# First mixer's output norm in a two-block layer: pairs of squares added on VectorE, one-column sums moved behind the last product, constant matmuls on TensorE around the norms

## The reference

```python
def rms_norm(x, g):
    y = x * rsqrt(mean(x * x, axis=-1) + EPS)
    return y * g

merged = sigmoid(ga) * y_conv + sigmoid(gb) * y_attn
mix_out = merged @ w_out                                  # 1024 x 1024
x = x + gt1 * rms_norm(mix_out, g_post_mix)               # first norm of this stretch
h2 = rms_norm(x, g_pre_mlp) * (1.0 + sc2) + sh2           # second norm of this stretch
ff = square(relu(h2 @ w_mlp_in)) @ w_mlp_out
x = x + gt2 * rms_norm(ff, g_post_mlp)
...                                                       # then the second layer
```

## Time and profile before

| | |
|---|---|
| median of 3 runs | 819.95 us (818.74 to 822.18) |
| the profiled execution | 821.43 us |
| its span, first to last instruction | 819.7 us |
| TensorE matmuls busy | 767.8 us, 94% |
| VectorE busy | 523.6 us, 64% |
| ScalarE busy | 379.1 us, 46% |
| mean granted TensorE clock | 0.948 of full speed |

### The profile page before, as it was taken

One profiled execution on the slowest core, in us unless ns is written; L12 is line 12 of the kernel. 1 busy time (PEld: TensorE's weight loads), 2 busy tenths in 40 slices (PEclk: granted clock), 3 DMA queues, 4 the chain that ended last, 5 costly groups with the idle time before them and its releaser, 6 DMA issues.

```text
span 819.7 us, 14006 instructions
## 1 busy us (share of the span) xinstructions
PE 767.8 (94%) x6051; PEld 731.6 (89%) x6051; DVE 523.6 (64%) x706; ACT 379.1 (46%) x520; POOL 68.7 (8%) x68
## 2 busy tenths in 40 slices
PE   3599999999979999999998999899799999999997
PEld 3499989999979999999997997687489999999997
DVE  4887677687346776644436898967655676555441
ACT  3453443543433555553434445577653554443441
POOL 1500111001000000000001000004000222221000
PEclk9599999999869999999998988999799999999999
DMA  8979666785413886575651451241606476654511
GB/s 343 364 255 338 200 208 210 249 272 194 152 52 112 254 272 201 193 240 172 205 162 52 155 157 50 62 145 52 205 9 198 136 226 204 205 190 147 192 40 52
DMA packets 123826, 146.01 MB, mean 178 GB/s; under 512 B 3988, under 2 KB 114804, under 8 KB 123764
## 3 DMA queue, kind: packets, MB, share of 16 engines
q1 hardware_dynamic: 122400, 143.32, 53.3%
q10 hardware_dynamic: 1364, 1.79, 0.6%
HBM read 144.05 MB, written 1.05 MB: 177 GB/s over the span
## 4 chain that ended last, share of the span: by engine, by line
PE 71%; DVE 16%; issue 5%; ACT 4%; DMA 2%; POOL 1%; POOLq 0%; SPq 0%; ACTq 0%; DVEq 0%
PE bank L576 59%; DVE w_lo L1420 4%; DVE mod_acc L1412 3%; ACT w_hi L1030 2%; DVE wide L1715 2%; PE bank L622 2%; DMA raw<-in_w_ada 2%; PE bank L603 1%; DVE score L1776 1%; DVE neg_max L1781 1%; PE bank L786 1%; PE bank L815 1%; PE bank L801 1%; PE bank L611 1%; PE bank L873 1%
## 5 line engine op out<-in xcount | busy, mean ns | idle before, releaser
L1420 DVE TENSOR_TENSOR w_lo<-raw,w_hi 128x2048 fp32r<-128x2048 f32 (+1 forms) x108 | 243.7, 2261 | 139.3 <-ACT w_hi L1030 139.2
L1030 ACT ACTIVATE w_hi<-raw 128x2048 fp32r<-128x2048 f32 (+1 forms) x110 | 206.5, 1883 | 230.8 <-PE bank L576 209.1
L576 PE MATMUL bank<-act_hi,w_hi 128*128 128x256 f32 x816 | 235.1, 288 | 5.6 <-ACT act_hi L1186 2.7
L576 PE MATMUL bank<-act_lo,w_hi 128*128 128x256 f32 x816 | 232.5, 285 | 0.7 <-DVE act_lo L1680 0.4
L576 PE MATMUL bank<-act_hi,w_lo 128*128 128x256 f32 x816 | 231.9, 284 | 1.3 <-DVE w_lo L1420 1.3
L576 PEld LDWEIGHTS bank<-act_hi,w_hi 128*128 128x128 f32 x816 | 159.0, 195 | 9.3 <-issue 8.2
L576 PEld LDWEIGHTS bank<-act_lo,w_hi 128*128 128x128 f32 x816 | 159.0, 195 | 1.9 <-DVE act_lo L1680 0.7
L576 PEld LDWEIGHTS bank<-act_hi,w_lo 128*128 128x128 f32 x816 | 158.5, 194 | 1.9 <-DVE w_lo L1420 1.9
L576 PE MATMUL bank<-hidden_hi,w_hi 128*128 128x256 f32 x432 | 121.3, 281 | 1.3 <-DVE wide L1980 1.3
L576 PE MATMUL bank<-hidden_hi,w_lo 128*128 128x256 f32 x432 | 121.1, 280 | 0.0
L576 PE MATMUL bank<-hidden_lo,w_hi 128*128 128x256 f32 x432 | 121.1, 280 | 0.0
(11 more groups left out here) (265 smaller groups left out, 974.5 us busy)
## 6 DMA issues: line engine op xcount, KB each, us to landing
raw<-in_w_in SPq DMA_DIRECT2D x31, 1024.0 KB, 5.8
raw<-in_w_ada SPq DMA_DIRECT2D x24, 1024.0 KB, 6.8
raw<-in_w_gate_up SPq DMA_DIRECT2D x22, 1024.0 KB, 5.1
raw<-in_w_mlp_in SPq DMA_DIRECT2D x16, 1024.0 KB, 5.4
raw<-in_w_mlp_out SPq DMA_DIRECT2D x16, 1024.0 KB, 5.4
raw<-in_w_out SPq DMA_DIRECT2D x8, 1024.0 KB, 6.9
raw<-in_w_down SPq DMA_DIRECT2D x8, 1024.0 KB, 5.0
raw<-in_w_down SPq DMA_DIRECT2D x4, 768.0 KB, 4.3
```

What stands on the lines that cost most here:

```text
L576: i = e.matmul(dst, lhs, rhs, start=start and k == 0 and m == 0 and n == 0, stop=stop and k == kt - 1 and n == 2, skip_group_check=True)
L1030: e.activation(w_hi[slot][:, 0:kt * n_cols], raw[i % N_RAW][:, 0:kt * n_cols], ACT.Copy).then_inc(hi_split, 1)
L1420: e.tensor_tensor(w_lo[slot][:, 0:kt * n_cols], raw[i % N_RAW][:, 0:kt * n_cols], w_hi[slot][:, 0:kt * n_cols].bitcast(F32), ALU.subtract) ...
```

## The change

The sums between products OUT1 + 2 and OUT1 + 3 are gone. VectorE adds the squares of pair 1 to those of pair 0 (`add_to_first(1)`, ahead of a w_lo split), and those of pair 2 on top (`add_to_first(2)`, behind that split); each addition is over 128 x 512 and raises `pair_added`. After product OUT1 + 3 TensorE sums pair 0, once both additions are made, and pair 3. `keep_busy` multiplies the identity by itself, 128 columns wide, into the first 128 columns of the bank that product MLP1 will start anew: eight times after the first spreading, once after each of the four pair sums of the second norm, five times after the second spreading. The results are not read. The count that `ffn_sums` waits for in the second layer is raised by the two additions.

```diff
--- before.py
+++ after.py
@@ -613,16 +613,24 @@
                 if last:
                     i.then_inc(sums_done, 1)
 
-            def sum_columns(i, n):
+            def sum_columns(i, n, ready=None):
 
                 pe.wait_ge(consts, 3)
-                pe.wait_ge(squared, squared_by[n] + i)
+                if ready is not None:
+                    pe.wait_ge(*ready)
+                else:
+                    pe.wait_ge(squared, squared_by[n] + i)
                 for tt in range(TT):
                     for k in (2 * i, 2 * i + 1):
                         t = e.matmul(bank[SUMS][:, tt:tt + 1], squares[:, k, tt * P:(tt + 1) * P], mean_of[:],
                                      start=k == 0 and tt == 0, stop=k == DT - 1, skip_group_check=True)
                 if i == DT // 2 - 1:
                     t.then_inc(col_summed, 1)
+
+            def keep_busy(n, o):
+
+                for _ in range(n):
+                    e.matmul(o[:, 0:P], ident[:], ident[:], start=True, stop=True, skip_group_check=True)
 
             def spread_rstd(n):
 
@@ -726,20 +734,22 @@
             modulation_sum(SHIFT2)
             modulation_sum(SCALE2)
             product(OUT1 + 2, start_bank(OUT1 + 2), act_hi, act_lo, ready_merged)
+            product(OUT1 + 3, start_bank(OUT1 + 3), act_hi, act_lo, ready_merged)
             pe.wait_ge(rms_set, 1)
-            sum_columns(0, 0)
-            sum_columns(1, 0)
-            product(OUT1 + 3, start_bank(OUT1 + 3), act_hi, act_lo, ready_merged)
-            sum_columns(2, 0)
+            sum_columns(0, 0, ready=(pair_added, DT // 2 - 2))
             sum_columns(3, 0)
             spread_rstd(0)
+            o, o1 = start_bank(MLP1), start_bank(MLP1 + 1)
+            keep_busy(8, o)
             pe.wait_ge(col_rms, 1)
             for i in range(DT // 2):
                 sum_columns(i, 1)
+                keep_busy(1, o)
             spread_rstd(1)
-
-
-            two_products(MLP1, start_bank(MLP1), start_bank(MLP1 + 1), act_hi, act_lo, ready_h2)
+            keep_busy(5, o)
+
+
+            two_products(MLP1, o, o1, act_hi, act_lo, ready_h2)
             for p in range(MLP1 + 2, MLP2):
                 product(p, start_bank(p), act_hi, act_lo, ready_h2)
                 if p == GATE2_SUM_AFTER:
@@ -953,7 +963,7 @@
 
 
             def ffn_sums(i):
-                sum_tiles((2 * i,), i == 0, i == DT // 2 - 1, (pair_added, i + 1))
+                sum_tiles((2 * i,), i == 0, i == DT // 2 - 1, (pair_added, DT // 2 - 2 + i + 1))
 
             for i in range(DT // 2):
                 product(OUT2 + i, start_bank(OUT2 + i), act_hi, act_lo, ready_mix2)
@@ -1591,6 +1601,13 @@
             dve.wait_ge(mod_set, 3)
             e.tensor_tensor(gain1[:], mod[:, GATE1 * DT:(GATE1 + 1) * DT], cols("g_post_mix", 0, DT), ALU.mult).then_inc(gains_set, 1)
 
+            def add_to_first(i):
+
+                dve.wait_ge(squared, squared_by[0] + i)
+                dve.wait_ge(pair_added, i - 1)
+                e.tensor_tensor(squares[:, 0:2, :], squares[:, 0:2, :], squares[:, 2 * i:2 * i + 2, :],
+                                ALU.add).then_inc(pair_added, 1)
+
             def add_pair(i, n_squared):
                 dve.wait_ge(squared, n_squared)
                 e.tensor_tensor(squares[:, 2 * i, :], squares[:, 2 * i, :], squares[:, 2 * i + 1, :],
@@ -1604,7 +1621,9 @@
             e.tensor_scalar(scale2[:], mod[:, SCALE2 * DT:(SCALE2 + 1) * DT], 1.0, None, ALU.add).then_inc(gains_set, 1)
             dve.wait_ge(gains_set, 4)
             e.tensor_tensor(scale2[:], scale2[:], cols("g_pre_mlp", 0, DT), ALU.mult).then_inc(gains_set, 1)
+            add_to_first(1)
             low_after(product_at[OUT1 + 2])
+            add_to_first(2)
 
             def column_reciprocal(n):
                 dve.wait_ge(col_rms, n + 1)
```

## The result

Over 15 runs of each kernel, taken on the same chips, the changed kernel takes 816.17 us in the median (813.88 to 819.81) against 821.32 (818.61 to 826.10). The ratio is 0.994 with a 95% interval of 0.992 to 0.996: faster by .6%, or some 4.9 us (3.3 to 6.6). Forecast were 3.45 us less, 816.5, in a range of 813.0 to 819.4. That 816.5 and 816.17 meet is in part luck: the forecast started from 819.95, the median of 3 runs before, which over 15 runs is 1.4 us higher, and the measured change is larger than the forecast one by about as much. The prediction also held a gain within .5% for likelier (.55) than one above it (.41); .6% came. The two profiled executions differ by 5.3 us (816.13 and 821.43), so their traces can stand for the medians.

The account below looks back on a forecast made before the run. TensorE's queue was taken to bound the kernel (71% of the chain). Terms -1.70 - 1.1 + .7 - 1.35 = -3.45 us, from the median of 819.95 to 816.5 us; 8-in-10 range 813.0 to 819.4.

Parts of the forecast that it names:

- step 1: Between the last two projections: the one-column sums leave TensorE's queue, -1.70 us in full.
- step 2: Two VectorE additions, .68 us each, around the w_lo split: no cost, .5 us of cover for the second.
- Rival D: Additions on VectorE come late and TensorE waits: up to +.7 us on any case; no own chance, folded into bounds.
- steps 3 and 4: Second norm: eight constants after the first spread free at full clock; with singles, sums end earlier, -1.1 us (+1.3 to -2.4).
- step 5: Before the MLP: five constants at half clock, the product queued behind them, +.7 us.
- step 6: MLP's first two products: clock returns about 2.1 us into the product instead of 5.0, -1.35 us.
- The bound of -2.1: MLP's first two products: the most they could gain, at full clock from the start, -2.1 us.
- Kept behind: After the MLP's first products: the gain is kept, splits and loads move along, VectorE's split has 4 us of cover.
- Rival A: Clock holds at full from the first norm into the MLP: -6.7 us, 813.2 us; chance .22.
- Rival B: Only the removed sums count, constants' cost paid back by the earlier return: -1.70 us, 818.2 us; chance .15.
- Rival C: Constants are a load, clock falling before or in the eight: net +1.25 us, 821.2 us; chance .15.

Follow-up runs that it names:

- experiment 11: Changed kernel without the two VectorE additions, TensorE summing all four pairs behind the last projection: 819.03 us, ratio .9976 to the kernel before.
- experiment 2: Kernel before plus the constants alone (eight, one after each pair, five), sums left between the last two products: 818.95 us, ratio .9979.
- 7: Changed kernel with the second modulation sum moved behind product OUT1 + 2: 814.86 us, ratio .9923 to the kernel before.
- Experiment 3: Changed kernel without the eight constants behind the first spread: 817.46 us, ratio .9965 to the kernel before.
- 5: Changed kernel without the single constant behind each pair of the second norm: 815.66 us, ratio .9951 to the kernel before.
- 8: Changed kernel with ten constants also behind the third norm's spread: 814.02 us, ratio .9915 to the kernel before.
- 6: Changed kernel with three constants behind each pair of the second norm instead of one: 816.84 us, ratio .9962 to the kernel before.
- experiment 9: Changed kernel with second modulation sum behind OUT1 + 2, ten constants at the third norm, no singles: 810.86 us, ratio .9885 to the kernel before.
- experiment 10: Changed kernel with the edits of 7 and 8, two constants before the first spread, twelve behind it, three per pair: 814.48 us, ratio .9930 to kernel before.
- experiments 1: Changed kernel without any constants, only the moved sums and two VectorE additions: 817.38 us, ratio .9967 to the kernel before.
- experiment 4: Changed kernel without the five constants before the MLP: 818.58 us, ratio .9974 to the kernel before.

## Why the prediction was right, and where its sizes were off

**The moved sums** (step 1, -1.70) are shown: experiment 11 gives them back as 1.73 us, and the stretch that holds them shrank by 1.99. The .3 more was not in the sum. It lies in the last projection. Behind 16 one-column records it took 5.76 us before, with its first matmul .20 us ahead of the second and the rest .118 apart; directly behind the other projection its matmuls are .113 apart. 47 x .0044 and .09 at its start make the .3. The same 5.76 us stand in experiment 2, which keeps the sums there, and in 7, where a modulation sum stands there. Why the spacing differs isn't shown.

**The additions** (step 2) were free with .34 us of cover (225.12 to 225.46), a little less than the .5 estimated. Rival D did not occur.

**The eight constants and the singles** (steps 3 and 4, -1.1): measured -.89, with the picture that was forecast: two groups at full clock, two at half, the fall 3.6 us behind the last of the eight (230.4 to 234.0). Experiment 3 shows that the eight do this and 5 that the singles don't. But it is not certain to happen: with the eight in place the clock fell at or before their start in 2, 7 and 8 (231.3, 226.6 and 229.4) and came back within them, and in 11 it fell among them and stayed down.

**The five** (step 5, +.7): +.67. All but the last of their ten records run at half clock, with the product queued behind them.

**The return** (step 6, -1.35): measured -2.77, and here the sum was too small by 1.4 us. The largest part is the time of the return. I let the clock come back 4.6 to 6.0 us after dense work begins with the spread, by three returns of before, and so 2.1 us into the product. It took 2.7 us in the changed kernel (238.1 to 240.8), so that the product started at full clock, and the half clock of the second norm lasted 6.8 us, where some 10 were forecast. Before, 21 of its spacings were at half, .213 us instead of .113: 2.1 us, where the sum had 1.35. Next, .5 us are a wait that the sum left out. Before, the second and the third matmul came .55 and .38 us behind the ones ahead of them (244.04, 244.59, 244.97), in place of .21 each:

```profile
244.59 0.58 PE L576 MATMUL bank<-act_lo,w_hi 128*128 128x256 f32 x1
244.97 0.42 PE L576 MATMUL bank<-act_hi,w_lo 128*128 128x256 f32 x1
```

The second needs the first low tile, which was written at 244.54 (an instruction of .48 us from 244.06). In the changed kernel the constants fill that time, and the second matmul follows the first by .21 us (240.96, 241.16). The last .2 us is only where the chain is cut: its piece begins at 241.20, when the last constant ends, and the first matmul already at 240.96. So .2 us of the +.67 of the five belong here. Against these parts stands .1 us by which the first matmuls of the changed kernel start slower than the rest.

The return time isn't fixed either. With the five constants it came 2.6 to 3.2 us behind the second spread in the changed kernel and in 7 to 11, but 1.4 in 6, and 4.3, 4.7 and 6.0 in 3, 2 and 5.

The bound of -2.1 was too small, for a reason of counting. The prediction took the piece of 13.00 us for 96 matmuls of which the records show 90, and set against it 10.9 us for 96 at full clock. The records are complete: they follow each other at .113 us without a gap, and the piece ends with its 90th matmul. The rate was right: where a piece has all 96, it takes 10.90 us (experiment 9). For 90 it is 10.2, as measured, and the bound becomes -2.8.

**Kept behind**: yes. The chain from there to the end has the same length, and the VectorE cover was enough.

**Rival A** had its wait, its place and its condition right, and the condition failed, also where it was forced (6, 10). The rule of the Trainium skill that long idle gaps send the clock down (TensorE: Matmul & The Clock Gate, "Why this matters for your kernels") would have given it; the trace of experiment 10, with TensorE busy 8.58 of 8.70 us before the fall at 232.1, goes against that rule if taken as the only cause. **Rival B** had the constants at nothing net; experiments 1 and 2 refute it, though on the stretches more firmly than on the medians. **Rival C** had the right danger: in experiment 2 the clock did fall before the eight. Its price was wrong there, since it let them run at half clock to no end, and in 2, 7 and 8 the clock came back 3.4 us after its fall. In 11 it did not, and spread to spread took 1.3 us more than in the kernel before. The low end of the falls, 3.1 us, was too high for it as well: in 7 the clock fell 2.3 us behind the last product matmul.

## What to carry to other kernels

Where TensorE waits for a norm, multiply constants in the wait, most of all right before the next dense stretch: they cost what they overrun (.7 us here) and start the clock's return earlier (2.4 us here). Not every execution gains, as experiment 11 shows. Don't put 4 us of one-column work together; split it with a product between, which costs nothing. Before a piece of the chain is taken for a whole product, look in the code which matmul raises the semaphore that ends it: here it was the 90th of 96.

## What the runs showed of the hardware that I had not expected

Constants at half clock can bring it back as fast as products: at 234.7, 3.3 us after the first of the eight in experiment 2, against 4.1 us behind the first product matmul in experiment 4. In experiment 11 they did not, though TensorE was busy for 13.56 of the 13.6 us at half. Falls and returns move by some us with the small shifts between these programs and executions: the first fall behind the last projection lies between 226.6 and 236.3. And among one-column sums neither one nor three constants per group kept the clock at 2.4 GHz, though TensorE hardly idled in the tenth kernel.

These moves are not the whole of the several us by which executions differ. From the sums behind the third norm's two products to the end, where all thirteen kernels do the same work, the traces have 366.6 to 372.0 us with 27.6 to 33.4 us of half clock in them, and the longest has the least half clock. What lengthens it stays open.
